# Late token tiles: their split transposes kept in scratch memory from the output stage, in an fp32 encoder layer on one core

## The reference

```
x = layer_norm(ALPHA * x + mixer(x, ...), ln1_g, ln1_b)
x = layer_norm(ALPHA * x + moe(x, ...),   ln2_g, ln2_b)

def moe(x, ...):
    scores = sigmoid(x @ w_router)              # 1024 -> 16
    ...                                         # one of 4 groups, top 2 in it, gates
    h = silu(x @ w_gate[e]) * (x @ w_up[e])     # 1024 -> 256, for the chosen experts
    y = (gates * h) @ w_down[e]                 # 256 -> 1024
    shared = (silu(x @ ws_gate) * (x @ ws_up)) @ ws_down
    return y + shared
```

## Time and profile before

| what | value |
|---|---|
| time, median of three runs | 1228.56 us (1227.27 to 1228.61) |
| the profiled execution: its time | 1226.40 us |
| its span in the trace | 1224.5 us |
| mean granted TensorE clock | 0.997 |
| TensorE busy | 1202.5 us (98%) |
| VectorE, ScalarE, GpSimd busy | 59%, 48%, 18% |
| DMA, mean over the span | 194 GB/s, 237.47 MB |

### The profile page before, as it was taken

How to read it: one execution, slowest core, us unless ns; L and a number is a source line. 1 busy time by engine, 2 the same in 40 slices (tenths; PEclk the granted TensorE clock), 3 DMA queues, 4 the chain that set the end, 5 groups by cost and what they waited for, 6 DMA issues and landing times.

```text
span 1224.5 us, 22218 instructions
## 1 busy us (share of the span) xinstructions
PE 1202.5 (98%) x8067; PEld 1079.7 (88%) x8067; DVE 726.1 (59%) x1794; ACT 588.5 (48%) x1460; POOL 214.9 (18%) x274
## 2 busy tenths in 40 slices
PE   8999999999999999999899999999999999999997
PEld 8999898888888888888777888899989999999895
DVE  3222355655565556555777778558856655665477
ACT  4332344544454445444553333144566665675565
POOL 1121001200120012001211211000123432343222
PEclk9999999999999999999999999999999999999999
DMA  9797684365436543667845332372999999999794
GB/s 271 202 310 239 149 200 100 79 159 140 100 79 162 138 100 79 158 166 219 258 150 198 123 121 95 110 286 72 333 315 270 272 289 284 269 278 303 184 334 162
DMA packets 162802, 237.47 MB, mean 194 GB/s; under 512 B 41328, under 2 KB 111216, under 8 KB 162672
## 3 DMA queue, kind: packets, MB, share of 16 engines
q1 hardware_dynamic: 147968, 183.42, 50.0%
q0 software_dynamic: 11776, 41.95, 14.2%
q10 hardware_dynamic: 2976, 11.01, 2.2%
HBM read 147.44 MB, written 59.02 MB: 169 GB/s over the span
## 4 chain that ended last, share of the span: by engine, by line
PE 85%; issue 6%; DVE 3%; DMA 2%; ACT 1%; POOL 1%; SPq 1%; DVEq 0%; POOLq 0%; ACTq 0%
PE bank L889 19%; PE bank L891 19%; PE bank L890 19%; PE bank L1017 9%; PE bank L1004 5%; PE bank L883 5%; PE bank L995 4%; PE bank L996 3%; PE bank L1151 2%; DMA raw_gu<-in_ln_b 1%; POOL Q L2424 1%; DMA raw_gu<-in_w_up 1%; DMA a_work<-in_x 0%; DVE d_work L2097 0%; SPq L603 0%
## 5 line engine op out<-in xcount | busy, mean ns | idle before, releaser
L1476 ACT ACTIVATE b_work<-b_work 128x256 f32<-128x256 f32 (+3 forms) x288 | 148.1, 514 | 234.0 <-DVE b_work L1892 233.9
L889 PE MATMUL bank<-xgT_hi,w_gu_hi 128*128 128x224 f32 (+1 forms) x704 | 196.1, 279 | 0.8 <-DVE xgT_lo L1947 0.5
L891 PE MATMUL bank<-xgT_hi,w_gu_lo 128*128 128x224 f32 (+1 forms) x704 | 194.7, 277 | 0.0
L890 PE MATMUL bank<-xgT_lo,w_gu_hi 128*128 128x224 f32 (+1 forms) x704 | 194.7, 277 | 0.0
L1901 DVE COPY b_work<-bank 128x256 f32<-128x256 f32 (+2 forms) x256 | 112.6, 440 | 116.5 <-PE bank L1004 115.6
L889 PEld LDWEIGHTS bank<-xgT_hi,w_gu_hi 128*128 128x128 f32 x704 | 134.9, 192 | 3.2 <-DVE xgT_lo L1947 1.4
L890 PEld LDWEIGHTS bank<-xgT_lo,w_gu_hi 128*128 128x128 f32 x704 | 135.0, 192 | 0.7
L891 PEld LDWEIGHTS bank<-xgT_hi,w_gu_lo 128*128 128x128 f32 x704 | 135.0, 192 | 0.0
L2424 POOL CAST Q<-Q 128x512 fp32r<-128x512 f32 x48 | 53.3, 1142 | 432.6 <-DVE w_k_lo L1831 226.1
L1004 PE MATMUL bank<-keep,b_work 128*128 128x128 f32 x608 | 114.6, 274 | 3.7 <-ACT b_work L1476 3.5
L1004 PEld LDWEIGHTS bank<-keep,b_work 128*128 128x128 f32 x608 | 79.2, 139 | 37.8 <-ACT b_work L1476 9.9
(11 more groups left out here) (237 smaller groups left out, 2848.4 us busy)
## 6 DMA issues: line engine op xcount, KB each, us to landing
raw_gu<-in_w_gate SPq DMA_DIRECT2D x32, 512.0 KB
raw_gu<-in_w_up SPq DMA_DIRECT2D x32, 512.0 KB
raw_d<-in_w_down SPq DMA_DIRECT2D x16, 1024.0 KB
Q<-stage_hi SPq DMA_DIRECT2D x96, 128.0 KB, 2.4
Q<-stage_lo SPq DMA_DIRECT2D x96, 128.0 KB, 2.4
o_scratch<-b_work SPq DMA_DIRECT2D x36, 264.0 KB, 3.2
c_work<-o_scratch SPq DMA_DIRECT2D x12, 792.0 KB, 5.2
wo_scratch<-a_work POOLq DMA_DIRECT2D x16, 512.0 KB, 4.5
```

What stands on the lines that cost most here:

```text
L889: nc.tensor.matmul(o, w_hi, x_hi, start=first, stop=False)
L890: nc.tensor.matmul(o, w_hi, x_lo, start=False, stop=False)
L891: return nc.tensor.matmul(o, w_lo, x_hi, start=False, stop=last)
L1476: nc.scalar.activation(prob[:, u % 2, 0:n], prob[:, u % 2, 0:n], ACT.Exp, scale=-1.0, bias=o[:, HD:HD + 1], accum_out=o[:, HD + 1:HD + 2])\
```

## The change

What six of the transposed tiles give is computed once instead of twice. For the tiles 6 to 11:

- In the output stage the two banks of a tile's transposes are split in addition to the copy for the router: ScalarE writes a high part (`late_high`, into free columns of `raw_gu`), VectorE a low part (`late_low`, into a new buffer `late_lo` or into tile 6 of `base`, which `late_parts` names), and SP stores both to a new scratch `t_scratch` (`store_late`, 2 x 512 KB a tile). VectorE's part for tile t-3 stands in step t, ahead of the statistics; that of tile 9 stands behind the norm of tile 11, those of tiles 10 and 11 behind the split of the first down weights. TensorE's transposes of a tile t > 6 wait for VectorE's part of the tile before (`t_lo`), since they overwrite its banks.
- The late steps load both parts (2 MB a step) into the operand buffers straight away, and have no transposes and no splits. Late step 0 is loaded when the gate and up part of an earlier routed step is done, 1 and 2 behind the shared down weights. The parts lie in memory with the two tiles of a step one behind the other, so the gate and up matmuls of these steps read their 256 columns as two pieces of 128. The loads of the summed rows have one more wait (the gate and up part of the second late step), since the late parts of tile 6's buffer lie in `base`.
- The steps 8 and 9 of the output stage, the last round of the loop, are written out on each engine.

```diff
--- before.py
+++ after.py
@@ -114,6 +114,9 @@
...
+    t_d = nc.dram_tensor("t_scratch", (LATE, 2, P, 2 * D), FP32, kind="Internal").ap()
...
@@ -245,7 +248,7 @@
...
-            phase.enter_context(nc.sbuf_tensor("Q4_space", [P, 2 * GT], FP32))
+            late_lo = phase.enter_context(nc.sbuf_tensor("late_lo", [P, D], FP32))
...
@@ -339,6 +342,13 @@
...
+        def late_parts(t):
+            hi = raw_gu_t[:, 3 * D:4 * D] if t in (TILES - 3, TILES - 1) else raw_gu_t[:, 2 * D:3 * D]
+            lo = base[:, 2 * EARLY, :] if t in (TILES - 3, TILES - 1) else late_lo[:]
+            return hi, lo
...
@@ -501,7 +511,7 @@
...
-            return xg2 if n in (1, EARLY + 1) else xg3 if n == LATE0 + 1 else xg1
+            return xg2 if n in (1, EARLY + 1, LATE0) else xg3 if n == LATE0 + 1 else xg1
...
@@ -782,6 +792,16 @@
...
+                if isinstance(t, int) and 2 * EARLY + 3 <= t < TILES - 1:
+                    store_late(t - 3)
+            def store_late(t):
+                n = t - 2 * EARLY
+                sp.wait_ge(S["t_lo"], n + 1)
+                for part, rows in enumerate(late_parts(t)):
+                    sp.dma_start(t_d[n // 2, part, :, D * (n % 2):D * (n % 2) + D], rows)\
+                      .then_inc(S["t_st1" if t in (TILES - 3, TILES - 1) else "t_st0"], 16)
...
@@ -801,6 +821,7 @@
...
                 if q == 1:
+                    store_late(TILES - 4)
...
@@ -810,6 +831,7 @@
...
+            store_late(TILES - 3)
...
@@ -817,6 +839,10 @@
...
+            store_late(TILES - 2)
+            store_late(TILES - 1)
+            sp.wait_ge(S["t_st0"], 128)
+            sp.wait_ge(S["t_st1"], 64)
...
@@ -847,17 +873,16 @@
...
             def load_late(n):
-                wait("xgT_made", (more * 2 + (EARLY + 4 + n)) * 2)
-                for h in range(2):
-                    sp.dma_start(xg[:, h, :], x1_d[ST * (EARLY + n) + P * h:ST * (EARLY + n) + P * h + P, :])\
-                      .then_inc(S["late_ld"], 16)
+                for part in range(2):
+                    sp.dma_start(plain(xg_of(LATE0 + n)[part][:]), t_d[n, part]).then_inc(S[f"late_ld{n % 2}"], 16)
+            sp.wait_ge(S["gx_made"], EARLY + 2)
             load_late(0)
             load_d(more * 2 + 3)
-            load_late(1)
             wait("wd_lo", more * 8 + 20)
             load_raw_d(ws_down)
-            for n in range(2, LATE):
+            wait("gx_made", more * 2 + (EARLY + 4))
+            for n in range(1, LATE):
                 load_late(n)
...
@@ -867,6 +892,7 @@
...
+            wait("gx_made", more * 2 + (EARLY + 5))
...
@@ -1087,9 +1113,7 @@
...
-                if n >= LATE0:
-                    pe.wait_ge(S["late_ld"], 32 * (n - LATE0 + 1))
-                elif n == EARLY:
+                if n == EARLY:
...
@@ -1141,6 +1165,8 @@
...
+                if isinstance(t, int) and t > 2 * EARLY:
+                    pe.wait_ge(S["t_lo"], t - 2 * EARLY)
                 transposes(x1s[:, s, :], banks, S["x1T_made"])
...
@@ -1172,16 +1198,19 @@
...
-                pe.wait_ge(S["xg_lo"], 2 * q + 2)
+                if n >= LATE0:
+                    pe.wait_ge(S[f"late_ld{(n - LATE0) % 2}"], 32 * ((n - LATE0) // 2 + 1))
+                else:
+                    pe.wait_ge(S["xg_lo"], 2 * q + 2)
...
@@ -1190,14 +1219,19 @@
...
+                if n >= LATE0:
+                    x_hi, x_lo = (w[:].rearrange("p (h k c) -> p k h c", h=2, k=KD) for w in xg_of(n))
...
+                    if n >= LATE0:
+                        o = o.rearrange("p (h c) -> p h c", c=P)
                     for k in range(KD):
+                        x = (x_hi[:, k], x_lo[:, k]) if n >= LATE0 else (x_hi[:, k, 0:rows], x_lo[:, k, 0:rows])
                         last = three(o, w_hi[:, k, P * f:P * f + P], w_lo[:, k, P * f:P * f + P],
-                                     x_hi[:, k, 0:rows], x_lo[:, k, 0:rows], k == 0, k == KD - 1)
+                                     x[0], x[1], k == 0, k == KD - 1)
...
@@ -1225,7 +1259,7 @@
...
-                last = n == LATE0 + LATE - 1
+                last = n >= LATE0 - 1
...
@@ -1251,11 +1285,10 @@
...
                             ddn(q - 1, 1 - s, half, n - 1)
-                            dxt(src, half, q + 1, n + 1)
-                among = {0: first, EARLY: first_routed, LATE0: first_late, LATE0 + 1: first_routed}.get(n)
+                among = {0: first, EARLY: first_routed, LATE0: first_late}.get(n)
...
@@ -1556,6 +1589,23 @@
...
+                if isinstance(t, int) and t >= 2 * EARLY:
+                    late_high(t, banks)
+            def late_high(t, banks):
+                n = t - 2 * EARLY
+                if n == 0:
+                    act.wait_ge(S["wg_lo"], KD - 2)
+                elif t == TILES - 3:
+                    act.wait_ge(S["wg_lo"], KD)
+                elif t == TILES - 1:
+                    act.wait_ge(S["t_st1"], 32)
+                else:
+                    act.wait_ge(S["t_st0"], 32 * min(n, 3))
+                hi, _ = late_parts(t)
+                for c in range(2):
+                    copy(hi[:, 512 * c:512 * c + 512].bitcast(FP32R), banks[c][:]).then_inc(S["t_hi"], 1)
...
@@ -2022,6 +2076,15 @@
...
+            def late_low(t, banks=bank[2:4]):
+                hi, lo = late_parts(t)
+                for c in range(2):
+                    dve.wait_ge(S["t_hi"], 2 * (t - 2 * EARLY) + c + 1)
+                    last = V.tensor_tensor(lo[:, 512 * c:512 * c + 512].bitcast(FP32R), banks[c][:],
+                                           hi[:, 512 * c:512 * c + 512], ALU.subtract)
+                last.then_inc(S["t_lo"], 1)
...
@@ -2040,6 +2103,8 @@
...
+                if isinstance(t, int) and t >= 2 * EARLY + 3:
+                    late_low(t - 3)
...
@@ -2127,18 +2193,17 @@
...
-                        z_moments(Z_BN[0])
                     xg_low(q + 1, 1, n + 1)
                 if n == LATE0 + 1:
+                    z_moments(Z_BN[0])
                     z_out(0)
...
@@ -2326,8 +2391,11 @@
...
+            late_low(TILES - 3)
             dve.drain()
             dn_split(0, 0)
+            late_low(TILES - 2, bank[5:7])
+            late_low(TILES - 1, bank[5:7])
             xg_low(1, 0, 1)
...
```

More of the change, by code:

```diff
@@ L791, in _ @@
             c_step(1, 1, lambda d: True)
-            with sp.Fori(0, TILES // 2 - 2) as i:
+            with sp.Fori(0, TILES // 2 - 3) as i:
                 for s in range(2):
                     c_step(2 * i + 2 + s, s, lambda d: True)
-            for t in range(TILES - 2, TILES):
+            for t in range(TILES - 4, TILES):
                 c_step(t, t % 2, lambda d, t=t: 0 <= t + d < TILES)
@@ L1606, in _ @@
                 gu_high(0, t - 2, gu1)
-            with act.Fori(0, TILES // 2 - 3) as i:
+            with act.Fori(0, TILES // 2 - 4) as i:
                 for s in range(2):
@@ L1610, in _ @@
                     gu_high(0, 2 * i + 2 + s, gu1)
-            for t in range(TILES - 2, TILES):
+            for t in range(TILES - 4, TILES):
                 c_step(t, t % 2, lambda d, t=t: 0 <= t + d < TILES, t)
+                if t < TILES - 2:
+                    gu_high(0, t - 2, gu1)
             def gu_split(q, s, n):
@@ L1728, in d_step @@
                     z_stats(2)
-                if not last and not soon and n >= EARLY:
+                if not soon and EARLY <= n < LATE0 - 1:
                     xg_high(q + 1, 0, n + 1)
@@ L1736, in d_step @@
                     xg_high(q + 1, 1, n + 1, bank[0:2])
-                elif not last and not soon and n >= EARLY:
+                elif not soon and EARLY <= n < LATE0 - 1:
                     xg_high(q + 1, 1, n + 1, bank[0:2] if n == EARLY + 1 else bank[2:4])
@@ L2060, in _ @@
                 c_step(t, t % 2, t // 2, lambda d, t=t: 0 <= t + d < TILES, t)
-            with dve.Fori(0, TILES // 2 - 3) as i:
+            with dve.Fori(0, TILES // 2 - 4) as i:
                 for s in range(2):
                     c_step(2 * i + 4 + s, s, i + 2, lambda d: True)
-            for t in range(TILES - 2, TILES):
+            for t in range(TILES - 4, TILES):
                 c_step(t, t % 2, t // 2, lambda d, t=t: 0 <= t + d < TILES, t)
@@ L2113, in d_step @@
                 last = n == LATE0 + LATE - 1
-                soon = n in (0, EARLY, LATE0, LATE0 + 1)
+                soon = n in (0, EARLY)
+                rows = not soon and n < LATE0 - 1
                 if n > LATE0 + 1:
@@ L2137, in d_step @@
                     z_out(1)
-                if not last and not soon:
+                if rows:
                     xg_low(q + 1, 0, n + 1)
                 h_low(q, s, n)
-                if not last and not soon:
+                if rows:
                     xg_low(q + 1, 1, n + 1, bank[0:2] if n == EARLY + 1 else bank[2:4])
@@ L2454, in _ @@
                 c_step(t, t % 2, lambda d, t=t: 0 <= t + d < TILES, t - 2 if t >= 2 else None)
-            with pool.Fori(0, TILES // 2 - 3) as i:
+            with pool.Fori(0, TILES // 2 - 4) as i:
```

(4 more changed lines are left out.)

15 lines of the change are left out of this document (8 added, 7 removed).

## The result

| | before | changed | ratio (95% interval) |
|---|---|---|---|
| median of six runs | 1227.91 us | 1235.37 us (1234.37 to 1236.88) | 1.0054 (1.004 to 1.0069) |
| profiled execution: time, span | 1226.40, 1224.5 us | 1235.92, 1234.1 us | |
| mean granted clock | 0.997 | 0.989 | |

A forecast was written before the change was run, and what follows sets the result against it. TensorE was taken as the bound (busy 98% of the span), with DMAs bounding the late end. 0.2 + 1.15 + 3.5 + 1.2 - 2.5 = +3.5 us on 1226.4 profiled, median 2.16 above: 1232.1 us, range 1227.0 to 1236.0.

The forecast's parts named there:

- Tiles 6 and 7: Output stage: VectorE's added splits of these tiles mostly fit into existing waits; +0.2 us in all.
- Shared step's start: Output stage: tile 8's copy and split delay tile 11's residual, so TensorE begins the first shared step 1.15 us later.
- Tile 9's split: Output stage: split stands behind tile 11's norm; TensorE's transposes of tile 10 wait for it, +3.5 us more.
- The clock: Behind the new TensorE gap near 800, the granted clock falls to half rate for 2 to 4 us; +1.2, bounds 0 and 2.
- Late end: Late steps: removed transposes and splits save 2.5 us at the end, limited by DMAs; bounds 0.5 and 5 us off.
- Matmuls in pieces: Late steps: 288 gate and up matmuls reading 256 columns as two pieces of 128 cost 0; bounds 0 and 9 us.
- Two of the marks: Expected in the profile after: a shift by 5 to 6 us between 805 and 1140; final statistics 5 to 8 us later.
- Rival 1: Clock stays up behind the output stage's gap: +2.3 us, 1230.9, no measurable change; 25%.
- rival 2: Faster, 1225.2: late gain whole, tile 10's wait 2.5 us; needs its transposes before 801.6, final statistics before 1172; 10%.
- rival 4: Late steps: matmuls in pieces are slower by 20 ns each, 5.8 us, cancelling the removal; about +6, 1234.6; 5%.
- Rival 3: DMAs a worse bound in the late steps: statistics at 1180 or later, end gains nothing or loses 1 us; 1235.2; 15%.

The follow-up runs named there:

- e7_behind: Changed kernel, but tile 10's transposes no longer wait for tile 9's split and tile 8's split moved behind tile 10's norm: 1225.27 us, ratio 0.997 to before.
- e3_late1: Changed kernel with late step 1's rows loaded first, ahead of the down weights' split wait and the shared down weights: 1230.89 us, ratio 1.0022 to before.
- e4_front: Only the output stage's part of the change; late steps as before the change, stored parts not read: 1236.99 us, ratio 1.0064 to before.
- e6_late12: Changed kernel with the rows of late steps 1 and 2 both loaded ahead of the shared down weights: 1229.9 us, ratio 1.0006 to before.
- e10_ln2first: Changed kernel with ln2's rows (1 MB) loaded ahead of the rows of late steps 1 and 2: 1239.06 us, ratio 1.0084 to before.
- e5_both: Changed kernel without the wait ahead of tile 10's transposes and with late step 1's rows loaded first: 1224.75 us, ratio 0.9963 to before.
- e8_all: Changed kernel with the edits of e7_behind and e6_late12 joined: 1223.06 us, ratio 0.9952 to before.
- e9_best: Changed kernel with the edits of e7_behind and e3_late1 joined: 1220.88 us, ratio 0.9944 to before.

## Why the prediction was right in its sign, and half in its size

By the changed kernel's trace, against its tile 0 (2.11):

- **Tiles 6 and 7, +0.2**: the residuals of tiles 8 and 10 start 1.57 and 1.82 us later than before, so +0.25. Ahead of them, from tile 0's 2.11 to 1.57, 0.54 us were gained, most of it where the loop now ends and step 8 is written out. That was not forecast, and no run tells its cause apart.
- **Shared step's start, +1.15**: 2.87 - 1.82 = 1.05. The chain of VectorE and ScalarE was read rightly, and e7_behind removes it.
- **Tile 9's split, +3.5**: 6.40 - 2.87 = 3.53, with a wait of 3.40 us. Right; in each of the five kernels that keep the wait, the transposes start 6.50 us after the shared step, whatever the clock does between.
- **The clock, +1.2, bounds 0 and 2**: 11.11 - 6.40 = 4.7. This is the term that failed. That it would fall was right, at somewhat better than even chances; how long it stays down was taken from one short fall at 618, of some 3.5 us. Here it was down for 10 us. What the fall costs can be read ahead of the routed steps, from the start of tile 10's transposes (799.01 before) to ScalarE's first silu of the shared steps (816.11 before): 11.02 - 6.40 = 4.6 us here. In the four other kernels with this wait it is 3.1 (e3_late1, e4_front and e6_late12) and 4.7 us (e10_ln2first), for 7 to 10 us at half clock: never under 2. The Trainium skill (TensorE: Matmul & The Clock Gate, Why this matters for your kernels) warned of idle gaps; the runs agree for this gap in all five. In the four others the clock had already fallen once, behind the 0.90 us wait; that first fall cost nothing by itself, since the transposes waited for the split anyway, and it made the idle stretch shorter (1.9 to 2.2 us instead of 3.40).
- **Late end, -2.5**: -1.6. The statistics came 12.36 - 11.11 = 1.25 us late (0.8 forecast), and from there to the last operation VectorE needed 40.78 us instead of 43.61, 2.8 less (3.3 forecast: the split, its wait and the wait for TensorE). So the mechanism, DMAs as the bound, stood: from the issue of the shared down weights (1161.22) to the landing of the last scatter-add (1170.11 + 11.96 = 1182.07) it took 20.9 us, 21.7 forecast. What the step missed lies just ahead of that issue: the prediction began its queue there, and did not ask whether loads behind it could go earlier. They could, since the DMA engines idled while SP waited for a split (the changed kernel, for the earlier trace rows):

```profile
1154.00:1156.00 2.00, 2.00 (x11) 1.38 (x10) 0.00 (x0) 1.26 (x2) 0.18 (x1) 1.00 0.08 31
1156.00:1158.00 2.00, 2.00 (x16) 1.82 (x15) 0.00 (x0) 1.19 (x3) 1.56 (x1) 1.00 0.00 0
```

It also called TensorE's saved time slack, where TensorE in fact stopped for late step 1's rows. Moved forward, the removal gives 6.1 to 6.2 us (e3_late1, e5_both, e6_late12), all of the 5.9, and 5.4 us in e8_all and e9_best.

- **Matmuls in pieces, 0**: right; they start 0.12 us apart in the late steps, as one piece does in the first shared step. From TensorE's timeline in late step 0:

```profile
1157.19 0.28 PE L917 MATMUL bank<-xgT_hi,w_gu_lo 128*128 128x256 f32 x1
1157.31 0.28 PE L915 MATMUL bank<-xgT_hi,w_gu_hi 128*128 128x256 f32 x1
```

Sum: 0.25 - 0.54 + 1.05 + 3.5 + 4.7 - 1.6 = 7.4 us. The profiled executions differ by 9.6; the other 2.1 us lie ahead of tile 0 and are a difference of executions. Two of the marks that the prediction set missed with the clock: against tile 0, the routed steps stand 9.0 us later (5 to 6 forecast) and the final statistics 10.25 us (5 to 8).

Rival 1 (clock stays) fell with the clock, rival 2 with the transposes at 805.41 and the statistics at 1188.97, rival 4 with the spacing. Rival 3 named nearly the measured time (1235.2), but by luck: it let the end gain nothing, and the end gained 1.6 us, while the clock took 3.5 us more than its 1.2.

## What to carry to other kernels

A wait that guards a buffer holds whatever stands in order behind it: ask for each use whether it touches that buffer at all; here the other banks needed none. A transfer's place in a queue is a dependency too: before calling a stage bound by bandwidth, look for windows in which the DMA engines idle just ahead of it. And price a new gap in TensorE's work at the gap plus the half clock behind it, with a spread from several falls, not from one.
